# The second layer's modulation: contraction blocks summed by VectorE, partitions added by TensorE

## The reference

```python
c_act, cctx_act = silu(c), silu(c_ctx)                      # two vectors of 1024
mod = c_act @ p['w_mod'] + p['b_mod']                       # 1024 x 6144, per layer
sh1, sc1, g1, sh2, sc2, g2 = jnp.split(mod, 6, axis=-1)
# last layer: the context tokens need only the first two of the six
mod_c = cctx_act @ p['w_mod'][:, :2 * D_MODEL] + p['b_mod'][:2 * D_MODEL]
h = rmsnorm(x) * (1.0 + sc1) + sh1
```

## Time and profile before

| | |
|---|---|
| median of three runs | 1298.62 us |
| profiled execution: span, first to last instruction | 1297.0 us (no other time of it is given) |
| TensorE matmul, weight load | 1239.0 us (96%), 997.2 us (77%) |
| VectorE, ScalarE | 706.1 us (54%), 521.4 us (40%) |
| GpSimd | 1.7 us |
| moved by DMA | 171.91 MB, mean 133 GB/s |
| mean granted TensorE clock | 0.989 of full speed |

### The profile page before, as it was taken

How to read it: one execution, slowest core, us unless ns; L and a number is a source line. 1 busy time by engine, 2 the same in 40 slices (tenths; PEclk the granted TensorE clock), 3 DMA queues, 4 the chain that set the end, 5 groups by cost and what they waited for, 6 DMA issues and landing times. The chain is left out here.

```text
span 1297.0 us, 18101 instructions
## 1 busy us (share of the span) xinstructions
PE 1239.0 (96%) x7532; PEld 997.2 (77%) x7532; DVE 706.1 (54%) x1206; ACT 521.4 (40%) x903; POOL 1.7 (0%) x8
## 2 busy tenths in 40 slices
PE   5999999999999899999999999999998998999997
PEld 3666767777676677777777788768877777999997
DVE  5654347958766734423222323556579777555554
ACT  4352445442544432222112222346555355543444
POOL 0000000000000000000000000000000000000000
PEclk9999999999999999999999999999999999999999
DMA  9833343431022264444544322313334213655653
GB/s 341 276 120 106 98 147 121 156 120 59 17 66 82 67 221 174 151 163 162 191 160 168 120 88 93 106 49 97 99 100 129 80 35 97 195 180 184 187 171 125
DMA packets 132457, 171.91 MB, mean 133 GB/s; under 512 B 9332, under 2 KB 112406, under 8 KB 132376
## 3 DMA queue, kind: packets, MB, share of 16 engines
q1 hardware_dynamic: 131892, 170.58, 40.8%
q10 hardware_dynamic: 484, 0.18, 0.1%
HBM read 169.69 MB, written 1.05 MB: 132 GB/s over the span
## 5 line engine op out<-in xcount | busy, mean ns | idle before, releaser
L1680 DVE TENSOR_TENSOR w_lo<-w_raw,w_hi 128x1024 fp32r<-128x1024 f32 (+1 forms) x220 | 264.1, 1204 | 318.1 <-ACT w_hi L1321 317.6
L1321 ACT ACTIVATE w_hi<-w_raw 128x1024 fp32r<-128x1024 f32 (+1 forms) x220 | 228.5, 1042 | 396.1 <-DMA w_raw<-in_w_gu_dram 182.9
L665 PE MATMUL ps<-h_hi,w_hi 128*128 128x512 f32 (+1 forms) x896 | 312.8, 349 | 4.0 <-ACT gate L1612 2.0
L666 PE MATMUL ps<-h_lo,w_hi 128*128 128x512 f32 (+1 forms) x896 | 304.7, 340 | 0.0
L667 PE MATMUL ps<-h_hi,w_lo 128*128 128x512 f32 (+1 forms) x896 | 304.5, 340 | 0.0
L665 PEld LDWEIGHTS ps<-h_hi,w_hi 128*128 128x128 f32 x896 | 171.2, 191 | 38.3 <-issue 20.1
L665 PE MATMUL ps<-f_hi,w_hi 128*128 128x512 f32 (+1 forms) x544 | 188.2, 346 | 5.7 <-DVE att_lo L2211 2.7
L667 PEld LDWEIGHTS ps<-h_hi,w_lo 128*128 128x128 f32 x896 | 171.2, 191 | 19.2
L666 PEld LDWEIGHTS ps<-h_lo,w_hi 128*128 128x128 f32 x896 | 171.5, 191 | 17.0
L667 PE MATMUL ps<-f_hi,w_lo 128*128 128x512 f32 (+1 forms) x544 | 183.4, 337 | 0.0
L666 PE MATMUL ps<-f_lo,w_hi 128*128 128x512 f32 (+1 forms) x416 | 140.3, 337 | 0.0
(11 more groups left out here) (308 smaller groups left out, 1566.4 us busy)
## 6 DMA issues: line engine op xcount, KB each, us to landing
w_raw<-in_w_gu_dram SPq DMA_DIRECT2D x88, 512.0 KB, 3.6
w_raw<-in_w_in_dram SPq DMA_DIRECT2D x60, 512.0 KB, 3.8
m_raw<-in_w_mod_dram SPq DMA_DIRECT2D x32, 512.0 KB, 4.9
w_raw<-in_w_down_dram SPq DMA_DIRECT2D x32, 512.0 KB, 3.5
m_even<-in_w_mod_dram SPq DMA_DIRECT2D x12, 1024.0 KB, 5.8
m_odd<-in_w_mod_dram SPq DMA_DIRECT2D x12, 1024.0 KB, 5.9
m_first<-in_w_mod_dram SPq DMA_DIRECT2D x16, 512.0 KB, 10.5
w_raw<-in_w_out_dram SPq DMA_DIRECT2D x16, 512.0 KB, 3.4
```

Source lines behind the costliest of these rows:

```text
L665: mm(o, w_hi[:, i % RING, w], hi[:, 0:n], start=first and k == 0, stop=False)
L666: mm(o, w_hi[:, i % RING, w], lo[:, 0:n], start=False, stop=False)
L1321: A(w_hi[:, i % RING, w], w_raw[:, i % RING, w], ACT.Copy).then_inc(w_hi_done, 1)
L1680: TT(w_lo[:, i % RING, w], w_raw[:, i % RING, w], w_hi[:, i % RING, w].bitcast(F32), ALU.subtract).then_inc(w_lo_done, 1)
```

## The change

The transfers stay as they are, but VectorE takes over the sum over the eight contraction blocks. A block of w_mod has 128 contraction rows on the partitions; the vector's 128 values are a scalar for each partition. add_mods(j) multiplies the first block by it and multiplies and adds the others into m_acc, for each stream: two (both vectors) for rows 0 and 1, one for the rest, which is 64 VectorE instructions of 128x1024 in all. What is left is the sum over the partitions: summed_rows(m) does it on TensorE with a column of ones (m_pick, 32 columns, of which one is ones), four matmuls of 256 columns for each stream. The sums sit in every other slot from 16 to 62, the rows in slots 24, 32, ... 64 and the turnings two slots behind. Transfer j is issued at slot 16+2j and waits for the sums of transfer j-2; before a row's first sum VectorE waits until TensorE has read the row before. Three clears of m_pick stand ahead of mods_read.

```diff
+MOD_SUMS = 16
+def mod_sum_at(v):
+    return (v - MOD_SUMS) // 2 if MOD_SUMS <= v < MOD_SUMS + 48 and v % 2 == 0 else None
 def mod_rows_at(v):
-    return v if v in (0, 1) else (v - 1) // 2 if 5 <= v <= 47 and v % 2 == 1 else None
+    m, left = divmod(v - MOD_SUMS - 8, 8)
+    return m if left == 0 and 0 <= m < 6 else None
 def mod_turn_at(v):
-    return MODS_FIRST + MODS_IN + (v - 9) // 8 if 9 <= v <= 49 and v % 8 == 1 else None
+    m = mod_rows_at(v - 2)
+    return None if m is None else MODS_FIRST + MODS_IN + m
+def mod_streams(m):
+    return 2 if m < 2 else 1
+def mod_adds(j):
+    return sum(2 * mod_streams(i // 4) for i in range(j))
...
             def load_big(j):
-                sp.wait_ge(m_used, KD * MODS_IN + max(j - 1, 0))
+                sp.wait_ge(m_used, KD * MODS_IN)
+                if j >= 2:
+                    sp.wait_ge(S["mod_added"], mod_adds(j - 1))
...
-                    if l == 0 and s in (9, 10):
-                        load_big(s - 9)
...
-                            v = ffn_slot(part, s) - RING
-                            if v >= 1 and mod_rows_at(v + 4) is not None:
-                                load_big(mod_rows_at(v + 4))
+                        if l == 0 and mod_sum_at(ffn_slot(part, s)) is not None:
+                            load_big(mod_sum_at(ffn_slot(part, s)))
...
-            def mod_pair(j):
-                pe.wait_ge(m_full[j % 2], 16 * (KD * MODS_IN // 2 + j // 2 + 1))
-                for i in range(2):
-                    k = 2 * (j % 4) + i
+            def summed_rows(m):
+                pe.wait_ge(S["mod_added"], mod_adds(4 * m + 4))
+                for s in range(mod_streams(m)):
                     for g in range(4):
-                        c0 = i * MOD_COLS + g * CW
-                        last = mm(ps[32 * g:32 * g + 32, MOD, CW:2 * CW], cact[:, k, :], m_big[j % 2][:, c0:c0 + CW],
-                                  start=(k == 0), stop=(k == KD - 1))
-                last.then_inc(m_used, 1)
+                        last = mm(ps[32 * g:32 * g + 32, MOD, CW:2 * CW], m_pick[:, s, :], m_acc[:, s, g * CW:(g + 1) * CW],
+                                  start=(s == 0), stop=(s == mod_streams(m) - 1))
+                p.sig(last, "rows_made")
...
             def copy_row(m):
-                j = m - MODS_FIRST + 1
-                act.wait_ge(m_used, KD * j if j <= MODS_IN else KD * MODS_IN + 4 * (j - MODS_IN))
+                if m < MODS_FIRST + MODS_IN:
+                    act.wait_ge(m_used, KD * (m - MODS_FIRST + 1))
+                else:
+                    p.after("rows_made")
...
                     read_mod(0, 16, MODB)
+                    p.chain(V.memset(m_pick[:], 0.0))
+                    p.link(V.memset(m_pick[:, 0, 0:1], 1.0))
+                    p.link(V.memset(m_pick[:, 1, 1:2], 1.0))
+                    p.settle()
                     p.sig(V.memset(sm[:, 2, 15:16], 0.0), "mods_read")
...
+                def add_mods(j):
+                    m = j // 4
+                    dve.wait_ge(m_full[j % 2], 16 * (KD * MODS_IN // 2 + j // 2 + 1))
+                    if j % 4 == 0 and m > 0:
+                        p.after("rows_made")
+                    for i in range(2):
+                        k = 2 * (j % 4) + i
+                        src = m_big[j % 2][:, i * MOD_COLS:(i + 1) * MOD_COLS]
+                        for s in range(mod_streams(m)):
+                            acc, by = m_acc[:, s, :], cact[:, k, s:s + 1]
+                            if k == 0:
+                                ins = TS(acc, src, by, None, ALU.mult)
+                            else:
+                                ins = STT(out=acc, in0=src, scalar=by, in1=acc, op0=ALU.mult, op1=ALU.add)
+                            p.sig(ins, "mod_added")
+                        p.own("mod_added")
...
+                            if l == 0 and mod_sum_at(v) is not None:
+                                add_mods(mod_sum_at(v))
```

More of the change, by code:

```diff
@@ L281, in backbone @@
         t_mask = at("t_mask", 169.5, [2, P])
+        m_acc, m_pick = at("m_acc", 152, [2, MOD_COLS]), at("m_pick", 205, [2, 32])
         m_first = [at(f"m_first{m}", kb, [2, MOD_COLS]) for m, kb in enumerate((80, 112, 120, 128, 136, 88, 96, 104))]
@@ L322, in backbone @@
             "x_transposed", "xT_ready", "x_rms", "rms_psum", "first_rstd", "vec_transposed", "cact_ready",
-            "eps_ready", "cact_cleared", "decay_rates", "dsel_ready", "mod_rows_copied", "first_mods", "row_ready", "row_turned", "mods_read",
+            "eps_ready", "cact_cleared", "decay_rates", "dsel_ready", "mod_rows_copied", "first_mods", "mod_added", "rows_made", "row_ready", "row_turned", "mods_read",
             "filt_psum", "spec_ready", "arg_ready", "sine_ready", "taps_read", "taps_ready", "spectra_psum",
@@ L330, in backbone @@
             "feat_psum", "f_hi_ready", "feat_read", "ssd_lo",
-            "qk_ready", "heads_squared", "head_ss", "head_rms", "heads_scaled", "heads_ready", "heads_transposed", "qkT_ready",
+            "qk_ready", "heads_squared", "head_ss", "heads_scaled", "heads_ready", "heads_transposed", "qkT_ready",
             "scores", "row_max", "probs_ready", "rec_ready", "turned_psum", "probT_act", "probT_dve", "pv_done", "o_ready",
@@ L533, in _ @@
                         load_w(g + s, src[:, 4 * half:4 * half + 4, col:col + CW], 4)
-                        if l == 0:
-                            v = ffn_slot(part, s) - RING
-                            if v >= 1 and mod_rows_at(v + 4) is not None:
-                                load_big(mod_rows_at(v + 4))
+                        if l == 0 and mod_sum_at(ffn_slot(part, s)) is not None:
+                            load_big(mod_sum_at(ffn_slot(part, s)))
                         if l == 0 and part == 0 and s == RING:
@@ L546, in _ @@
                         load_w(g + s, src[:, 2 * c0 + k0:2 * c0 + k1, (s // 3) * CW:(s // 3 + 1) * CW], k1 - k0)
[L547 to L550, removed]
+                        if l == 0 and mod_sum_at(ffn_slot(part, 4 * n + s)) is not None:
+                            load_big(mod_sum_at(ffn_slot(part, 4 * n + s)))
             for t in range(2):
@@ L648, in mods_in_ffn @@
                 if mod_rows_at(v) is not None:
-                    mod_pair(mod_rows_at(v))
+                    summed_rows(mod_rows_at(v))
             def pair_open(q):
@@ L2289, in _ @@
                             residual(l, f"down{part}", s // 3 - 1, 40, n)
+                        if l == 0 and mod_sum_at(ffn_slot(part, 4 * cnt + s)) is not None:
+                            add_mods(mod_sum_at(ffn_slot(part, 4 * cnt + s)))
                     if part == 1:
```

## The result

| | before | after |
|---|---|---|
| median of 4 runs each, one chip | 1298.84 us (1298.24 to 1300.48) | 1277.59 us (1277.3 to 1278.92) |
| profiled execution: time, span | -, 1297.0 us | 1277.61, 1275.8 us |
| TensorE, VectorE busy | 1239.0, 706.1 us | 1216.1 (95%), 781.1 us (61%) |
| mean granted clock | 0.989 | 0.988 |

The ratio is 0.9837 (0.9823 to 0.9852): faster, by some 21 us. The forecast was 1279.8. All ratios are of fast executions, which leaves out two slow ones beside the experiments, of c0_again (3419.43 us) and of the kernel before (1743.07 us), without which their medians are 1280.42 and 1299.32, not 1281.57 and 1299.45.

The account below looks back on a forecast made before the run. TensorE's issued stream was taken to bound layer 0's feed-forward from about 463 us. Stream -20.6, clears +0.3 and clock +1.5 gave -18.8 us, so 1279.8 us; range 1277.0 to 1284.0.

Parts of the forecast that it names:

- The stream: TensorE in layer 0's feed-forward: 29.35 us of pair steps and turnings go, 8.78 come, so 20.6 us shorter.
- The sums: VectorE in layer 0's feed-forward: 64 instructions of 1.28 us, 82 us in all, hidden behind TensorE at cost 0.
- Rival B: VectorE sums cost near 1.9 us each, slots 16 to 31 lose 3.6 us, time 1283.4; chance 0.10.
- The round: VectorE in slots 16 to 31: sums, splits and hidden product take 17.6 of TensorE's 21.8 us per four pieces.
- Waits for mod_added, rows_made and splits: New waits of TensorE and VectorE in layer 0's feed-forward: cost 0, up to 2.6 us if a sum came late.
- The move of the 24 loads: The 1 MB loads move from slots 0 to 47 to slots 16 to 62: weights still arrive in time, cost 0.
- Rival D: Weights and transfers really set the pieces' rhythm, the 20.6 us is given back, time 1300.4; chance 0.02.
- The clears: Three small clears of m_pick ahead of mods_read in the output stage: +0.3 us on the path, ends 0 and 0.9.
- The clock: Longer TensorE idle ahead of layer 0's feed-forward lowers the granted clock behind it: +1.5 us, ends 0 and 1.7.
- rival A: The clock does not fall at 439 us, ahead of layer 0's feed-forward: time 1278.3; chance 0.20.
- rival E: Clock changes further on, as in layer 1, fall differently: 1 to 3 us either way; no chance of its own.

Follow-up runs that it names:

- c0_again: The changed kernel run again unedited on another chip: 1281.57 us with its slow execution, ratio 0.9858 to the kernel before.
- e5: Changed kernel with 56 of the 64 VectorE sums cut to 8 columns in place of 1024: 1278.86 us, ratio 0.9849.
- e3: Changed kernel with each VectorE sum of rows 0 and 1 done twice, once into scratch: 1290.85 us, ratio 0.994.
- e6: Changed kernel with dummy matmuls at slots 0 and 1, clears moved behind mods_read, five turnings put beside the next row's step: 1278.9 us, ratio 0.9846.
- e1: Changed kernel with two steps of eight unread dummy matmuls at slots 0 and 1, ahead of layer 0's feed-forward: 1278.29 us, ratio 0.9841.
- e2: Kernel before the change with only its first two pair steps moved from slots 0 and 1 to 2 and 3: 1300.98 us, ratio 1.0011.
- e8: Changed kernel with only ScalarE's first gate of layer 0's feed-forward moved ahead of a weight rounding: 1278.1 us, ratio 0.9845.
- e4: Changed kernel with each VectorE sum of rows 2 to 5 done twice, once into scratch: 1279.03 us, ratio 0.985.
- e7: e6 plus ScalarE's first gate of layer 0's feed-forward moved ahead of a weight rounding: 1274.58 us, ratio 0.9819.

## Why the prediction came out right

- **The stream.** -20.6 predicted, -20.62 measured behind the first 96, and 352.93 to 352.98 in five kernels with the changed program there. All prices were distances between starts of the same shapes, and all came back. This carries almost all of the result.
- **The sums.** 1.28 us predicted for the scalar form at 1024 columns, from a line through 256 and 512 columns; 1280 and 1283 ns measured. The eight opening multiplications were taken at the same price and take 752. VectorE's total is 76.4 us, not 82, and hidden either way (e5). Rival B is out. The round that this was set against (17.6 of 21.8 us) adds busy times and leaves out the residual steps in slots 24 to 35; e3 shows both, and neither mattered at this size.
- **Waits for mod_added, rows_made and splits.** None on TensorE. VectorE waited twice for rows_made, 3.7 us in all, and nobody waited for it. The move of the 24 loads cost nothing that a wait shows. Rival D is out: no weight is late.
- **The clears.** +0.3 predicted, 0.86 - 0.53 = 0.33 measured, and e6 takes it back.
- **The clock.** It fell, so rival A is out; e1 and e2 show that the missing pairs are why. But the term is mis-sized for the profiled execution: 1.5 was read from layer 1, and 2.47 us were lost in the first 15 products. The reason is in the windows: in layer 1 the low stretch covered 3.45 us of work, here 1.59 + 2.00 + 2.00 = 5.59, and the prediction's own formula on these windows gives 1.59 x 0.50 + 2.00 x 0.50 + 2.00 x 0.43 = 2.66. What I missed as well is that TensorE's next wait, for the gate, takes up 0.8 of it. Net 1.7, inside the ends 0 and 1.7 only because two errors met. Nor is 2.47 the one right value: the loss over the first 15 was 1.58 in c0_again and 1.32 in e8, near the 1.5, and 2.4 to 2.7 in the other five traces without matmuls in the gap. Two steps of matmuls in the wait were worth 1.0 to 1.7 us. The Trainium skill's "TensorE: Matmul & The Clock Gate", Part 1, by which activity is what lifts the clock from its throttled default, agrees with e1 and e2.
- **The 2.2 us below the forecast.** The steps sum to -20.6 + 0.3 + 1.7 = -18.6. Layer 1 gave another -2.58 and the end -0.57, and +0.56 came ahead of the feed-forward beside the clears: together -21.2. The last three are no part of the change's working, and in another execution they add up otherwise; that the time lies 2.2 below the forecast is, as far as the runs show, luck: c0_again lies 0.6 above it, e4 and e5 0.8 and 0.9 below. In layer 1 the windows of 20 us that hold a drop (TensorE busy, clock) are three in before,

```profile
890.00:910.00 20.00, 20.00 (x141) 0.91 0.40 109
...
950.00:970.00 20.00, 18.15 (x118) 0.91 0.32 90
...
1010.00:1030.00 20.00, 17.80 (x121) 0.91 0.26 79
```

and one in after:

```profile
950.00:970.00 20.00, 16.22 (x110) 0.91 0.30 88
```

That is rival E, which the prediction gave 1 to 3 us either way. It isn't a gain of the change: c0_again, the same program, has three drops and 243.51. Over the twelve traces the stretch takes 243.2 on average with three drops (5 traces), 241.9 with two (3), 240.7 with one (4), about 1.3 us for each. The ratio of c0_again, 0.9858, is 18.5 us on its 1299.45, and those of e4 and e5, whose stage is after's to 0.04 us, are 19.5 and 19.6 on 1298.7. These are nearer to the 18.6 of the steps, though their intervals hold 21.2 as well.

What sets the number of drops in layer 1 stays open. It differs between traces of one program, so it isn't the program alone, and no run here tests a cause. The same holds for the stretch ahead of the feed-forward.

## What to carry to other kernels

Where TensorE's stream is full, price each step by the distance between neighbouring starts, over a stretch long enough to hold the slower products behind a switch; that gave three costs right to 0.01 us. Do the same for the engine that is to be hidden behind it: busy times made VectorE's sums 1.28 us where they are 1.20 apart. Before work is taken out of a wait, look at the granted clock behind it: the work may be what keeps the clock up, and dummy matmuls can stand in for it. A gain of one or two us in one stage must be read in that stage, since the clock elsewhere moves the total by more.

## What the runs showed that was not expected

- Every kernel without matmuls in that gap (after, c0_again, e2, e3, e4, e5, e8) stood idle 4.4 us and then ran the first products slowly; none with them did. How long it stayed slow differs for one and the same program: 15 products took 5.99 us in after and 5.10 in c0_again, against 3.52 at full clock.
- Ahead of layer 1's feed-forward TensorE is idle for 2.75 us in all twelve traces, and in all of them the granted clock falls to its low level at most about 1 us before or behind the first product there. The 2.51 us idle ahead of layer 0's, in before, e1, e6 and e7, never brought that. No run put matmuls into layer 1's gap.
- Where TensorE waits in full work, a low clock can follow and cost more: in e3 it fell behind two of the waits, of 2.4 and 3.9 us. The 1.5 us behind the second came on top; at the first VectorE was the bound, and TensorE had the time to lose.
- tensor_scalar with a scalar for each partition takes 752 ns for 1024 columns of float32, where scalar_tensor_tensor takes 1280 and tensor_tensor 1223.
- Sums of 8 columns still take 222 ns, so some 0.2 us of a sum isn't its columns.
